# Projections from a normalised residual, in a new order of column blocks, in a two-layer hybrid block

## The chip, the cores and the metric

The kernel runs on one core of a Trainium2 chip. Its engines are TensorE (PE in the profile; PEld is its weight load), VectorE (DVE), ScalarE (ACT), GpSimd (POOL) and SyncE (SP), which here only issues transfers. The metric is the device time of one execution in microseconds; lower is better.

## The reference

Two layers, each with three token mixers side by side, then a gated feed-forward part, on 256 tokens of width 1024, all in float32. Cut to what matters:

```python
for l in range(2):
    h = rms_norm(x, norm_mix[l])              # x * rsqrt(mean(x*x) + 1e-6) * weight
    proj = h @ w_in[l]                        # 1024 -> 7688 columns
    (dq, dk, dv, dz, da, db, mq, mk, mv, lx, ly, gates) = split_columns(proj)
    # DeltaNet: conv4+silu on dq, dk, dv; chunked gated delta rule; rms_norm, times silu(dz)
    y_dn = gated_deltanet(dq, dk, dv, dz, da, db, ...) @ dn_out[l]
    y_mb = moba_attention(mq, mk, mv) @ mb_out[l]      # rope, causal softmax attention, 4 heads
    y_lru = rg_lru_branch(lx, ly, ...) @ lru_out[l]    # conv4, gates, linear scan, gelu(ly)
    g = sigmoid(gates + b_gate[l])                     # 3 x 1024 columns
    x = x + (g0 * y_dn + g1 * y_mb + g2 * y_lru) @ w_o[l]
    h = rms_norm(x, norm_ffn[l])
    gate, up = split(h @ ffn_in[l]);  x = x + (silu(gate) * up) @ ffn_down[l]
return rms_norm(x, norm_final)
```

## The kernel before

All weights come as one stream of 292 half blocks of 128 x 1024 float32 (512 KB each), 146 steps in each layer. A step k uses half block m = 146 l + k. Five buffers (`RING`) hold it raw; ACT rounds it to `whi` (`hi`, L676), DVE takes the rest into `wlo` (`lo`, L909), and PE makes three products (high x high, high x low, low x high). The activations are split the same way into `ahi` and `alo`. Both splits run four steps ahead (`AHEAD`): in step k, ACT and DVE prepare half block k + 4, and the buffer is free when PE is through with step k - 1.

Steps 0 to 59 of a layer are the input projection, two steps for each of 30 blocks of 256 columns. `by_output` (L292) keeps the weights stationary and streams 256 tokens: 24 matmuls of 128 x 256 in a step. `z_tokens` (L408; steps 32 to 35, the columns dz) keeps the tokens stationary and streams 512 columns: 12 matmuls of 128 x 512 in a step. Steps 60 to 71 are the three output products (y), 72 to 79 are w_o, 80 to 145 the feed-forward part, by tokens.

Nothing is scheduled by a tool: the order on each engine is written by hand. Each engine runs over the steps k, and a function `side(l, k)` holds what it does in step k besides the stream: on PE after the step's own matmuls, on ACT after rounding block k + 4, on DVE before `lo` of block k + 4. So one late operation holds back all that stands behind it on its engine, and also the weights of step k + 4.

The norm is applied late. PE projects x times the norm's weight; `evacuate` (L1038, the tensor operation at L1046) multiplies each pair of tiles by the tokens' reciprocal roots (`rstd`) on its way from PSUM to `proj`. The roots come from a sum of squares (`squares`, L707, on ACT) and `rsqrt` (L911, on DVE, with `settle()` waiting for each operation), and `norm_spread` (L431) spreads them over the partitions. Before layer 0, x comes transposed from memory (`xt_in`, `first_norm`); before layer 1, PE transposes it (`x_transpose`, L399) between the last matmuls of the layer ahead.

The DeltaNet work that the prediction speaks of, with its old steps: the column `conv` (L946) and silu of the six blocks of dq, dk, dv (`CONV_AT`); cumulative gates (`grow`, L1086, for PE in step 9); the table of decays E1 (differences at L1108, minimum, exponent at L729, steps 12 and 13); transposes of k and q and the squares of their rows (L737, steps 13 and 14); `kend` (L743, step 16); the inverse of the triangular matrix in five rounds of two products (`level`, `xcopy`, L1159, steps 18 to 27). The two products that give the attention its values by tokens are the transposes `mvT` (step 28).

Of the kernel before, what the change touches and what calls it, by code (L numbers as in the profile page):

```python
# [38 lines left out]

TQ, TK, TV, TMQ, TMK, TMV, TLX, TLY, TZ, TG = 0, 4, 8, 12, 16, 20, 24, 28, 32, 36  # L40
# [18 lines left out]
for _n, _k in [("ident", 128), ("causal", 128), ("fold", 8), ("cos", 256), ("sin", 256), ("tri", 128), ("eye", 64),  # L59
               ("up1", 64), ("up2", 64), ("up4", 64), ("up8", 64), ("up16", 64), ("up32", 64)]:  # L60
    CON[_n] = _at
    _at += _k
# [28 lines left out]
def build(nc, wstream, params, consts, norms, final, x_in, xt_in, ab_in, out, known):  # L91
    ctx = ExitStack()
    with ctx:
# [15 lines left out]
        con = sb("con", [P, NCON])  # L109
        par = sb("par", [P, NPAR])  # L110
        nrm = sb("nrm", [P, 2 * L * KT])
        rstd = sb("rstd", [P, T])
# [8 lines left out]
        small = sb("small", [P, 306])  # L121
# [5 lines left out]
        loaded_xt = [sem(f"loaded_xt{i}") for i in range(4)]  # L127
        loaded_x, loaded_final = sem("loaded_x"), sem("loaded_final")
# [5 lines left out]
        signals = (PE, DV, AC)  # L134
# [12 lines left out]
        for name, n in [("gcol", 8), ("bcol", 8), ("egc", 8), ("kes", 4), ("mx", 8), ("rs", 8),  # L147
                        ("brh", 4), ("bih", 4), ("bgh", 24), ("sp2", 4), ("sp4n", 4), ("nwh", 1), ("anex", 4), ("hr", 2), ("s2r", 2),
# [5 lines left out]
        assert at <= 306  # L154
# [20 lines left out]
        SQJ = 48  # L175
        PR, PT, VTOK = 48, 54, 8
        S1, WB, VN0, VN1, O1, OJ, OZ, ZT = 36, 16, 18, 38, 20, 8, 4, 4
        XC, TR, TI, A0, UU, HS = 12, 52, 0, 24, 20, 52
        MIX = 0
        XT, JUNK, FINAL, XW = 52, 44, TZ, 8  # L180
# [26 lines left out]
        CONV_AT = (5, 6, 7, 9, 11, 15)  # L207
# [17 lines left out]
        def in_bank(c):  # L225
            return bank[4 + c if c < 2 else c % 2]

        ZC = 16

        def is_z(k):  # L230
            return ZC <= k // 2 < ZC + 2

# [9 lines left out]
        def _(sp):  # L242
# [4 lines left out]

            sp.dma_start(nrm[:, :], norms).then_inc(loaded_nrm, 16)
            for p in range(4):
                sp.dma_start(tiles(XT + 2 * p, 2), xt_in[:, 2 * p:2 * p + 2, :]).then_inc(loaded_xt[p], 16)  # L250
                if p < 2:
                    load(p)
            sp.dma_start(rab[:, :, :, :], ab_in).then_inc(loaded_ab, 16)
            load(2)
            load(3)
            sp.dma_start(x[:, :, :], x_in).then_inc(loaded_x, 16)
            load(4)
            sp.dma_start(con[:, :], consts).then_inc(loaded_con, 16)
            for l in range(L):

                if l:
                    sp.wait_ge(*AC.at(l - 1, ("gates", 29)))
                    sp.wait_ge(*DV.at(l - 1, ("mixed", 3)))
# [7 lines left out]
            for t in (1, 0):  # L271
                for c in range(2):
                    sp.wait_ge(*(DV.at(L, ("out", t)) if c else AC.at(L, ("out", t))))
                    sp.dma_start(out[:, t, c * 512:(c + 1) * 512], x[:, t, c * 512:(c + 1) * 512]).then_inc(stored, 16)
# [4 lines left out]
        def _(pe):  # L279
# [12 lines left out]
            def by_output(l, k, dst, start_kt, act_wait=None):  # L292

                for i in range(4):
                    kt = start_kt + i
                    if act_wait is not None:
                        act_wait(kt)
# [92 lines left out]
            def turn_hidden(l, j):  # L390

                for t in range(2):
                    pe.wait_ge(*DV.at(l, ("hid", j, t)))
                    for f in range(2):
                        ins = pe.transpose(bank[3][:, f * T + t * P:f * T + (t + 1) * P],  # L395
                                           proj[:, HID + 2 * (j % 2) + t, f * P:(f + 1) * P], c_("ident", P))
                ins.then_inc(*PE.up(("hT", j)))

            def x_transpose(l, step, t):  # L399

                for c in range(2):
                    pe.wait_ge(*DV.at(l, (step, "x", t, c)))
                    for kt in range(4 * c, 4 * c + 4):
                        ins = pe.transpose(xt_of(kt)[:, t * P:(t + 1) * P], x[:, t, kt * P:(kt + 1) * P], c_("ident", P))
                        if kt % 2:
                            ins.then_inc(*PE.up((step, "xT", t, kt // 2), l))

            def z_tokens(l, k):  # L408

                m, q = l * NH + k, k - 2 * ZC  # L410
# [1088 lines left out]
```

## Time and profile before

| | us |
|---|---|
| median of 3 runs | 965.54 (964.45 to 967.15) |
| the profiled execution | 964.58, of it span 962.8 |
| PE busy | 935.2 (97% of the span), 6444 matmuls |
| DVE busy | 687.6 (71%) |
| ACT busy | 474.2 (49%) |
| POOL busy | 0.2 |
| weights and inputs read | 157.65 MB, 165 GB/s over the span |
| mean granted TensorE clock | 0.991 |

The chain of work that ended last goes 84% of its length through PE, 11% through DVE, 2% through ACT and 1% through a transfer. A row of a timeline has the start in us, the duration in us, the engine, the line and the operation with what it writes and reads; in brackets stands how long the engine had been idle and what ended that. Matmuls overlap, so their durations say little; their starts do.

### The profile page before, as it was taken

The numbers are of one execution on the slowest core, as the hardware profiler recorded it, in microseconds if no ns is written. First come the engines' busy times: TensorE is split into PE (matmuls) and PEld (weight loads), VectorE is DVE, ScalarE is ACT, GpSimd is POOL, SyncE is SP. The second block draws the span as 40 slices with busy tenths as digits, with TensorE's granted clock in tenths as the row PEclk, the third lists the DMA queues.
The fourth block names the chain that finished last, engine by engine and source line by source line (L and its number), as shares of the span: only waits on it lengthen the run. The fifth ranks groups of instructions, "written<-read, shape, count | busy, mean of one in ns | idle before, by whom it ended". The sixth has DMA issues, their size and how long they took to land.

```text
span 962.8 us, 15536 instructions
## 1 busy us (share of the span) xinstructions
PE 935.2 (97%) x6444; PEld 842.4 (87%) x6444; DVE 687.6 (71%) x1095; ACT 474.2 (49%) x769; POOL 0.2 (0%) x4
## 2 busy tenths in 40 slices
PE   7998999999999999999999899999999999999996
PEld 4998998999987888888889899999999788888884
DVE  4999976796777555555679998759758675565555
ACT  5554253975446444444454533558644464444442
POOL 0000000000000000000000000000000000000000
PEclk9999999999999999999999999999999999999998
DMA  9543433365564655565644343334655555555541
GB/s 339 169 139 131 133 109 115 130 194 199 167 196 147 210 180 197 175 204 187 201 137 132 126 133 132 123 120 135 215 189 181 178 196 197 181 183 187 180 145 44
DMA packets 44278, 159.71 MB, mean 166 GB/s; under 512 B 5040, under 2 KB 5168, under 8 KB 44080
## 3 DMA queue, kind: packets, MB, share of 16 engines
q1 hardware_dynamic: 44208, 158.72, 49.8%
q8 instruction: 51, 0.84, 0.4%
q14 instruction: 19, 0.16, 0.0%
HBM read 157.65 MB, written 1.05 MB: 165 GB/s over the span
## 4 chain that ended last, share of the span: by engine, by line
PE 84%; DVE 11%; ACT 2%; DMA 1%; issue 1%; SPq 0%; DVEq 0%; ACTq 0%
PE bank L282 11%; PE bank L283 10%; PE bank L284 10%; PE bank L382 8%; PE bank L380 8%; PE bank L381 8%; PE bank L429 6%; PE bank L322 5%; PE bank L323 5%; PE bank L324 5%; DVE tmp L952 3%; DVE wlo L909 3%; DMA x<-x_dram 1%; PE bank L395 1%; DVE proj L1046 1%; PE bank L418 1%
## 5 line engine op out<-in xcount | busy, mean ns | idle before, releaser
L676 ACT CAST whi<-raw 128x1024 fp32r<-128x1024 f32 x292 | 305.8, 1051 | 387.9 <-PE bank L284 152.6
L909 DVE TENSOR_TENSOR wlo<-raw,whi 128x1024 fp32r<-128x1024 f32 x292 | 353.5, 1219 | 115.8 <-ACT whi L676 115.7
L282 PE MATMUL bank<-ahi,whi 128*128 128x256 f32 x896 | 260.3, 291 | 0.7 <-DVE alo L977 0.6
L283 PE MATMUL bank<-alo,whi 128*128 128x256 f32 x896 | 254.7, 284 | 0.0
L284 PE MATMUL bank<-ahi,wlo 128*128 128x256 f32 x896 | 254.5, 284 | 0.0
L282 PEld LDWEIGHTS bank<-ahi,whi 128*128 128x128 f32 x896 | 173.1, 193 | 3.7 <-DVE alo L977 0.8
L283 PEld LDWEIGHTS bank<-alo,whi 128*128 128x128 f32 x896 | 173.2, 193 | 0.2
L284 PEld LDWEIGHTS bank<-ahi,wlo 128*128 128x128 f32 x896 | 173.0, 193 | 0.0
L380 PE MATMUL bank<-whi,ahi 128*128 128x512 f32 x320 | 126.5, 395 | 0.0
L382 PE MATMUL bank<-whi,alo 128*128 128x512 f32 x320 | 124.9, 390 | 0.0
L381 PE MATMUL bank<-wlo,ahi 128*128 128x512 f32 x320 | 124.6, 389 | 0.0
L382 PEld LDWEIGHTS bank<-whi,alo 128*128 128x128 f32 x320 | 60.1, 188 | 12.8
L381 PEld LDWEIGHTS bank<-wlo,ahi 128*128 128x128 f32 x320 | 60.2, 188 | 12.0
L380 PEld LDWEIGHTS bank<-whi,ahi 128*128 128x128 f32 x320 | 60.1, 188 | 11.9
L322 PE MATMUL bank<-whi,bhi 128*128 128x512 f32 x160 | 62.5, 390 | 0.0
L324 PE MATMUL bank<-whi,blo 128*128 128x512 f32 x160 | 62.3, 389 | 0.0
L323 PE MATMUL bank<-wlo,bhi 128*128 128x512 f32 x160 | 62.3, 389 | 0.0
L284 PE MATMUL bank<-bhi,wlo 128*128 128x256 f32 x192 | 54.4, 283 | 0.0
L282 PE MATMUL bank<-bhi,whi 128*128 128x256 f32 x192 | 54.3, 283 | 0.0
L283 PE MATMUL bank<-blo,whi 128*128 128x256 f32 x192 | 54.3, 283 | 0.0
L1352 DVE TENSOR_TENSOR blo<-bank,bhi 128x512 fp32r<-128x512 f32 x22 | 15.2, 692 | 40.3 <-ACT bhi L867 40.3
L1345 DVE SCALAR_TENSOR_TENSOR proj<-proj,bank 128x256 f32<-128x256 f32 x44 | 18.4, 418 | 35.4 <-ACT proj L863 35.4
(248 smaller groups left out, 1212.2 us busy)
## 6 DMA issues: line engine op xcount, KB each, us to landing
raw<-stream_dram SPq DMA_DIRECT2D x292, 512.0 KB, 4.0
par<-params_dram SPq DMA_DIRECT2D x2, 568.5 KB, 9.7
proj<-xt_dram SPq DMA_DIRECT2D x4, 256.0 KB, 6.3
x<-x_dram SPq DMA_DIRECT2D x1, 1024.0 KB, 10.6
out_dram<-x SPq DMA_DIRECT2D x4, 256.0 KB, 2.6
con<-consts_dram SPq DMA_DIRECT2D x1, 676.0 KB, 12.3
proj<-final_dram SPq DMA_DIRECT2D x1, 512.0 KB, 6.1
rab<-ab_dram SPq DMA_DIRECT2D x1, 64.0 KB, 7.4
```

Of the source, the lines that this page charges most:

```text
L282: pe.matmul(dst, whi_of(m)[:, wcol], hi, start=first, stop=False, skip_group_check=True)
L283: pe.matmul(dst, whi_of(m)[:, wcol], lo, start=False, stop=False, skip_group_check=True)
L284: return pe.matmul(dst, wlo_of(m)[:, wcol], hi, start=False, stop=last, skip_group_check=True)
L322: pe.matmul(dst, hi[:, tok], whi_of(m)[:, col], start=first, stop=False, skip_group_check=True)
L323: pe.matmul(dst, hi[:, tok], wlo_of(m)[:, col], start=False, stop=False, skip_group_check=True)
L324: ins = pe.matmul(dst, lo[:, tok], whi_of(m)[:, col], start=False, stop=False, skip_group_check=True)
L380: pe.matmul(dst, ahi[:, kt, tok], whi_of(m)[:, col], start=kt == 0, stop=False, skip_group_check=True)
L381: pe.matmul(dst, ahi[:, kt, tok], wlo_of(m)[:, col], start=False, stop=False, skip_group_check=True)
L382: ins = pe.matmul(dst, alo[:, kt, tok], whi_of(m)[:, col], start=False, stop=kt == KT - 1, skip_group_check=True)
L429: return pe.matmul(dst, lhsT, rhs, start=start, stop=stop, skip_group_check=True)
L676: act.copy(whi_of(m), raw_of(m)).then_inc(*AC.up(("hi", m), "w"))
L909: dv.tensor_tensor(wlo_of(m), raw_of(m), whi_of(m), ALU.subtract).then_inc(*DV.up(("lo", m), "w"))
```

## The change

- The order of blocks in the stream changes. z comes first (steps 0 to 3), then the blocks in the order of `AT`: dk, mq, dk, mq, dq, mk, dq, mk, dv, ly, dv, then mv (steps 26 to 29), lx, ly, lx and the gates. Blocks that feed a convolution alternate with blocks that don't.
- z and mv are computed by tokens. z goes through all four steps for tokens 0 to 127 and then for tokens 128 to 255. The eight transposes `mvT` are dropped.
- x is multiplied by its reciprocal root before it is transposed and split (`root`, `x_scaled`, `mix_norm`), in both layers, one half of the tokens after the other. `rstd`, `norm_spread` and the multiplication in `evacuate` are dropped; so is the transposed copy of x in memory. The root's Newton steps use one operation less each.
- With no scaling left, projections are read from PSUM by their consumers: the taps and the convolution, the gates' tanh, and plain copies by ACT (`in`, L842 of the new kernel).
- The products for da, db move from step 1 to step 3. Most side steps move: kk stays at 15, qT from 13 to 20, qk from 16 to 21, vT from 17 to 28, the inverse starts at 19 for 18, attention scores go from 26 to 31, the LRU part shifts by some five steps.
- The table of decays: ACT subtracts (eight activations with a bias), GpSimd sets what is above the diagonal (`affine_select`), then ACT takes the exponent. The copies `xcopy`, `xn` and the state go from DVE to ACT.
- The end: each half's root has its own chain, and the halves' stores change order.

```diff
+ROOT = -1.0 / 8192
+MV0 = 26
+CONVS, LX = (2, 3, 0, 1, 4, 5), (12, 13)
+AT = {2: 4, 6: 6, 3: 8, 7: 10, 0: 12, 8: 14, 1: 16, 9: 18, 4: 20, 14: 22, 5: 24, 12: 30, 15: 32, 13: 34}
+AT.update((c, 2 * c) for c in range(18, 30))
+FM = sorted(AT, key=AT.get)
-        CONV_AT = (5, 6, 7, 9, 11, 15)
+        CONV_AT = tuple(AT[c] + 2 for c in CONVS)
+            def z_tokens(l):
+                for t in range(2):
+                    for q in range(4):
+                        if t == 0:
+                            wait_split(l, q)
+                        ins = token_half(l, q, q, t, bank[4 + t][:, :])
...
+                        if t == 0 and q == 2:
+                            x_transpose(l, "mix", 1)
...
                     elif c < C_IN:
-                        if c > 3 and half == 0:
-                            pe.wait_ge(*DV.at(l, ("zs", c - ZC - 2) if ZC + 2 <= c < ZC + 4 else ("evac", c - 2)))
+                        n = FM.index(CHUNK[c])
+                        if n > 1 and half == 0:
+                            by, name = in_copied(FM[n - 2])
+                            pe.wait_ge(*by.at(l, name))
+            def mix_norm(l):
+                for c in range(2):
+                    if l == 0:
+                        act.wait_ge(loaded_x[0], 16)
+                    else:
+                        act.wait_ge(*DV.at(l, ("mix", "x", 0, c)))
+                    square(l, 0, c)
+                hi(l * NH + AHEAD - 1 if l else 0)
+                x_scaled(l, 0)
+                x_round(l, "mix", 2 * l, 0, (0, 1))
...
                 if k == 12:
-                    act.wait_ge(*DV.at(l, "dif"))
-                    act.activation(wide(E1, 4), wide(E1, 4), ACT.Exp).then_inc(*AC.up())
...
+                    act.wait_ge(*PE.at(l, "gbc"))
+                    for g in range(8):
+                        act.activation(wide(E1, 4)[:, g, :], b3(4 + g // 4, 4)[:, g % 4, :], ACT.Identity, bias=sm["gneg"][:, g:g + 1]).then_inc(*AC.up("dif"))
+                if k == 13:
+                    act.wait_ge(*PO.at(l, "causal"))
+                    act.activation(wide(E1, 4), wide(E1, 4), ACT.Exp).then_inc(*AC.up("decays"))
+            def root(l, t, order=(0, 1)):
...
+                for three in (3.0, 12.0, 768.0):
+                    settle()
+                    step(dv.scalar_tensor_tensor(out=u, in0=y, scalar=w, in1=y, op0=ALU.mult, op1=ALU.mult))
+                    settle()
+                    step(dv.scalar_tensor_tensor(out=y, in0=u, scalar=-three, in1=y, op0=ALU.add, op1=ALU.mult), ("mix", "nr", t))
-            def evacuate(l, k):
...
-                    step(dv.tensor_tensor(tiles(2 * c, 2), in_bank(c)[:, :].rearrange("p (a b) -> p a b", a=2),
-                                          over(rstd[:, :], 2), ALU.mult), ("evac", c))
+        @block.gpsimd
+        def _(po):
+            for l in range(L):
+                PO.layer = l
+                po.wait_ge(*AC.at(l, "dif"))
+                po.affine_select(wide(E1, 4), wide(E1, 4), [[0, 8], [1, P]], ALU.is_ge, -1e4, base=0, channel_multiplier=-1).then_inc(*PO.up("causal"))
```

The three places of the order on which the prediction leans. First ACT at the very start, before: L687 is the split of the transposed x, L708 the squares.

```order
L687 ACT_TABLE_LOAD
L687 ACTIVATE ahi<-proj,nrm 128x256 x2
L676 CAST whi<-raw 128x1024
L687 ACTIVATE ahi<-proj,nrm 128x256 x2
L676 CAST whi<-raw 128x1024
L687 ACTIVATE ahi<-proj,nrm 128x256 x4
L676 CAST whi<-raw 128x1024 x2
L708 ACTIVATE proj,small<-x 128x1024 x2
L676 CAST whi<-raw 128x1024
L714 CAST wab<-rab 128x8x8
```

The squares stood behind the split of x; nothing but the small product waited for them. The same place now: L710 squares, L724 x times its root, L719 the split.

```order
L710 ACT_TABLE_LOAD
L710 ACTIVATE proj,small<-x 128x512 x2
L707 CAST whi<-raw 128x1024
L724 ACTIVATE proj<-x,small 128x512
L719 ACTIVATE ahi<-bank,nrm 128x128 x2
L707 CAST whi<-raw 128x1024
L719 ACTIVATE ahi<-bank,nrm 128x128 x4
L707 CAST whi<-raw 128x1024
L719 ACTIVATE ahi<-bank,nrm 128x128 x2
L710 ACTIVATE proj,small<-x 128x512 x2
L707 CAST whi<-raw 128x1024
L724 ACTIVATE proj<-x,small 128x512
```

Now the squares and the root stand ahead of all the splits. Second, ACT around steps 12 to 15 of a layer, before: L729 the exponent, L737 the squares of the rows of k and q, L763 a tap.

```order
L729 ACTIVATE proj<-proj 128x1024
L730 ACTIVATE small<-small 128x4
L731 ACTIVATE small<-small 128x8
L676 CAST whi<-raw 128x1024
L737 ACTIVATE proj,small<-bank 128x128 x8
L676 CAST whi<-raw 128x1024
L737 ACTIVATE proj,small<-bank 128x128 x8
L763 ACTIVATE tmp<-proj,par 128x256 x2
L676 CAST whi<-raw 128x1024
```

The same place now: L808 the differences, L842 a copy of a block, L812 the exponent, L818 squares, L778 a tap, L804 the tanh of a convolution.

```order
L808 ACTIVATE proj<-bank,small 128x128 x8
L809 ACTIVATE small<-small 128x8
L842 COPY proj<-bank 128x512
L707 CAST whi<-raw 128x1024
L812 ACTIVATE proj<-proj 128x1024
L818 ACTIVATE proj,small<-bank 128x128 x8
L778 ACTIVATE tmp<-bank,par 128x256 x2
L707 CAST whi<-raw 128x1024 x2
L804 ACTIVATE tmq<-tmp 128x512
```

The exponent waits for GpSimd, and the taps of the third convolution stand behind it. Third, POOL in the new kernel, with what its rows wait for; in the old one it has only the first rows, up to the memsets.

```order
L1553 MEMSET const-uint8-127 128x1
L1446 UNCONDITIONAL_BRANCH [waits barrier_Pool_Activation_PE_DVE_SP_gather]
L1451 ISA [waits scalar_done]
L1451 AFFINE_SELECT proj<-proj 128x1024
L1451 AFFINE_SELECT proj<-proj 128x1024 [waits scalar_done]
L102 UNCONDITIONAL_BRANCH
```

One row without a tensor (ISA; in the built program it asks for the engine's library of functions) stands between the first wait for ACT and the first select, layer 0's. Layer 1's select has none ahead of it.

## Rows read from the trace of the kernel before

**Rows 1.** Who waited for whom on PE: total, times, longest, in us.
```profile
PE bank L446 <- DVE wab L1052: 4.7, 1, 4.7
PE bank L429 <- ACT Kend L743: 4.4, 2, 2.9
PE bank L429 <- DVE small L1086: 3.6, 2, 1.8
...
PE bank L429 <- DVE proj L1159: 1.2, 1, 1.2
```

**Rows 2.** Stretches: length, each engine's busy time and instructions, granted clock, DMA share, GB/s.
```profile
8.91:30.16 21.25, 16.50 (x121) 14.73 (x119) 13.86 (x34) 11.98 (x18) 0.00 (x0) 0.92 0.90 357
30.16:87.17 57.01, 53.69 (x459) 53.08 (x458) 54.22 (x128) 32.35 (x83) 0.00 (x0) 0.97 0.40 127
30.16:272.77 242.61, 238.06 (x2143) 232.26 (x2143) 200.72 (x329) 125.50 (x232) 0.00 (x0) 0.99 0.45 148
500.56:743.36 242.80, 238.04 (x2144) 232.37 (x2143) 200.74 (x329) 125.52 (x232) 0.00 (x0) 0.99 0.45 147
190.00:270.00 80.00, 80.00 (x669) 80.00 (x668) 62.26 (x70) 43.63 (x54) 0.00 (x0) 1.00 0.57 187
332.00:347.00 15.00, 15.00 (x68) 12.41 (x67) 9.06 (x11) 6.58 (x9) 0.00 (x0) 1.00 0.55 179
```

**Rows 3.** Groups by line and shape: count, then busy us, mean ns, idle before.
```profile
L909 DVE TENSOR_TENSOR wlo<-raw,whi 128x1024 fp32r<-128x1024 f32 x292 | 353.5, 1219 | 115.8 <-ACT whi L676 115.7
L1046 DVE TENSOR_TENSOR proj<-bank,rstd 128x512 f32<-128x512 f32 x56 | 38.2, 685 | 6.5 <-PE bank L284 6.2
...
L952 DVE SCALAR_TENSOR_TENSOR tmp<-proj,par,tmp 128x255 f32<-128x255 f32 x24 | 10.5, 480 | 0.0
...
L438 PE MATMUL bank<-con,proj 128*128 128x128 f32 x80 | 10.5, 274 | 0.0
```

**Rows 4.** Timeline of ACT: the first 20 us, then eight squares of step 13.
```profile
4.20 1.28 ACT L687 ACT_TABLE_LOAD   x1 [4.20 <-DMA proj<-xt_dram]
...
6.55 1.05 ACT L676 CAST whi<-raw 128x1024 fp32r<-128x1024 f32 x1 [0.15 <-DMA raw<-stream_dram]
...
16.55 1.06 ACT L708 ACTIVATE proj<-x 128x1024 f32<-128x1024 f32 x1 [1.44 <-DMA x<-x_dram]
...
66.13 0.27 ACT L737 ACTIVATE proj<-bank 128x128 f32<-128x128 f32 x1
...
67.89 0.31 ACT L737 ACTIVATE proj<-bank 128x128 f32<-128x128 f32 x1
```

**Rows 5.** Timeline of DVE: masks and first transpose of step 16; a root's chain.
```profile
79.37 1.78 DVE L1139 TENSOR_TENSOR proj<-bank,proj 64x256 f32<-64x256 f32 x4
...
84.40 2.32 DVE L909 TENSOR_TENSOR wlo<-raw,whi 128x1024 fp32r<-128x1024 f32 x2
...
493.40 0.16 DVE L914 TENSOR_SCALAR small<-small 128x2 f32<-128x2 f32 x1
...
495.38 0.16 DVE L923 SCALAR_TENSOR_TENSOR small<-small 128x2 f32<-128x2 f32 x1
```

**Rows 6.** Timeline of PE where layer 0 ends and layer 1 begins.
```profile
480.20 0.39 PE L337 MATMUL bank<-whi,blo 128*128 128x512 f32 x1
...
486.28 0.36 PE L282 MATMUL bank<-ahi,whi 128*128 128x256 f32 x1 [0.62 <-DVE alo L977]
```

**Rows 7.** Timeline of ACT at the square root of the LRU part.
```profile
190.59 1.28 ACT L830 ACT_TABLE_LOAD   x1
191.88 1.06 ACT L830 ACTIVATE proj<-proj 128x1024 f32<-128x1024 f32 x1
```

**Rows 8.** The page, DMA issues: count, KB each, median us to landing.
```profile
raw<-stream_dram SPq DMA_DIRECT2D x292, 512.0 KB, 4.0
```

**Rows 9.** Timeline of DVE at the end of the program.
```profile
954.84 0.16 DVE L1010 TENSOR_TENSOR small<-small 128x2 f32<-128x2 f32 x1 [0.26 <-ACT proj L887]
...
957.50 1.41 DVE L1027 SCALAR_TENSOR_TENSOR x<-x,small,proj 128x512 f32<-128x512 f32 x2
```

More of the change, by code:

```diff
@@ L270, in _ @@
                         sp.dma_start(flat(tiles(FINAL, 4)), final).then_inc(loaded_final, 16)
[L271 to L274, printed above, removed]
+            for t, c in ((0, 0), (1, 0), (1, 1), (0, 1)):
+                sp.wait_ge(*(DV.at(L, ("out", t)) if c else AC.at(L, ("out", t))))
+                sp.dma_start(out[:, t, c * 512:(c + 1) * 512], x[:, t, c * 512:(c + 1) * 512]).then_inc(stored, 16)
             sp.wait_ge(stored, 64)
@@ L707, in squares, with ffn_norm, wab_hi @@
+            def ffn_norm(l):
+                for t in range(2):
+                    x_round(l, "ffn", 2 * l + 1, t, range(KT))
+                for t in range(2):
+                    squares("ffn", t)
+            def wab_hi(l):
+                if l == 0:
+                    act.wait_ge(loaded_ab, 16)
+                act.copy(wab[:, :, 0:8], rab[:, l, :, :]).then_inc(*AC.up("wabh"))
             def squares(step, t):
@@ new lines, in x_scaled, with mix_update, add @@
+            def x_scaled(l, t):
+                settle()
+                step(dv.tensor_scalar(flat(tiles(XS + 4 * t + 2, 2)), x[:, t, 512:D], sm["nr"][:, t:t + 1], None, ALU.mult), ("xs", t))
+            def mix_update(l):
+                def add(t, c):
+                    if l:
+                        x_add(l, "mix", NH - 1, t, c)
+                add(0, 0)
+                add(0, 1)
+                root(l, 0)
+                x_scaled(l, 0)
+                if l == 0:
+                    lo(0)
+                add(1, 0)
+                x_split(l, "mix", 2 * l, 0, (0, 1))
+                if l == 0:
+                    lo(1)
+                add(1, 1)
+                x_split(l, "mix", 2 * l, 0, (2, 3, 4, 5))
+                if l == 0:
+                    lo(2)
+                x_split(l, "mix", 2 * l, 0, (6, 7))
+                root(l, 1)
+                x_scaled(l, 1)
+                lo(l * NH + AHEAD - 1)
+                x_split(l, "mix", 2 * l, 1, range(KT))
@@ L1025, in last_update @@
[L1025 to L1028 removed]
+                root(L, 1, (1, 0))
+                weighed(1)
+                weighed(0)
             def rnorm(l, name):
@@ L1189, in side @@
                                                      in1=Vb[:, 2 * h + 1, :], op0=ALU.mult, op1=ALU.add), "w")
-                if k == 36:
-                    for t in range(2):
-                        dv.wait_ge(*AC.at(l, ("tz", t)))
-                        step(dv.scalar_tensor_tensor(out=flat(tiles(TZ + 2 * t, 2)), in0=flat(tiles(ZT + 2 * t, 2)), scalar=1.0,
-                                                     in1=bank[t][:, :], op0=ALU.add, op1=ALU.mult), ("zs", t))
-                if k == 37:
+                if k == 38:
                     dv.wait_ge(*PE.at(l, "qs"))
```

678 lines of the change are left out of this document (328 added, 350 removed), and 2 rows, old and new, of the table at.

## The prediction

> **What bounds the kernel now.** I read the page first: PE is busy for 935.2 of 962.8 us, so time can only come from fewer matmuls or from the 27 us in which PE stands. Then the waits of PE [rows 1]. They are few and all lie in the two norms and in steps 4 to 19: 4.7 us at the very start (the products for da, db, behind the squares of x), 3.6 in two waits on `grow`, 4.4 in two on `Kend` (1.5 in layer 0, 2.9 in layer 1), 1.2 on one `xcopy`. Third, stretches [rows 2]. From step 4 to w_o a layer takes 242.6 and 242.8 us. Its first part, to step 19, is where DVE is busy 54.2 of 57.0 us: there DVE sets the pace, in the rest PE does. The granted clock is 1.00, full speed, in the stretches where PE never stops (190 to 270, 332 to 347), 0.97 in the early steps and 0.92 at the start, where PE had stood for those 4.7 us. What a clock of c costs in a stretch is (1 - c) of its length: 1.7 us in each of these two. Last the pace: 669 matmuls of 256 columns in 80 us, 0.120 each, 2.9 us for a step of 24; 68 matmuls of 512 columns in 15 us, about 0.225, 2.7 us for a step of 12 [rows 2].
>
> **PE's work.** mv by tokens: four steps at 2.7 for 2.9, -0.6 us a layer with rounding. The eight transposes `mvT` go; 80 such took 10.5 us [rows 3], eight with their filling some 0.9. The fold of da, db comes from step 3 into the stretch after step 4 (+0.5). So a layer's stretch from step 4 has 0.9 us less of pure work.
>
> **DVE's and ACT's work.** DVE loses `evacuate`, 28 x 0.68 = 19 us a layer [rows 3], and three kinds of copies to ACT. Where DVE sets the pace (steps 4 to 18) nine of them go, 6.1 of 54 us, and about 2 more with the differences, so the two `grow` waits should go. It helps only if DVE waits for nothing else, so I walk both engines through the new order, in us from the start of step 4, signals at zero cost. A `lo` is 1.2, a convolution of six operations 2.5 [rows 3], a block's copy by ACT 0.6, a rounding 1.0; eight squares take 2.0 (67.89 less 66.13 is seven of them [rows 4]); masks and first transpose 5.0 [rows 5].
> Up to step 12, nothing waits: convolution 0 ends at 9.6 and is wanted at 12.1, the log chain ends at 14 and is wanted at 20.8. PE starts step 12 at 24.8, 13 at 28.5, 14 at 31.4, 15 at 34.3, 16 at 38.9, 17 at 41.8, 18 at 44.7, 19 at 47.6, and would start 20 at 51.6. ACT has the differences at 27.1. Then GpSimd's select takes P. The exponent (1.0), eight squares (2.0) and the taps of step 14 (0.8) stand behind it on ACT, so with P = 2 the taps are there at 32.9, 1.5 after the block they read. Behind them on DVE stand convolution 2 (to 35.4), rope and `lo` (37.6), the scaling of the decays (39.4) and `lo` (40.6), silu, rope and `lo` (43.5), the masks (48.5), `lo`, convolution 3 (52.0), rope and two `lo`, silu 3 (56.0). PE wants convolution 2 at 38.9, the masks' transpose at 50.5, convolution 3 at 51.6 and silu 3 for the transposes of q at 54.5. So PE waits 0.4 + 1.1 = 1.5 us. DVE makes none of it up, since its `lo` is bound to the step that runs. The same walk with P = 4, 6, 8 gives 3.7, 5.6, 7.5: from 2 on, each us of select costs PE almost a us. From step 21 on I find no wait up to w_o; the closest places are the last round of the inverse (step 27: ready at 85.6, wanted at 86.3) and the square root, below.
>
> **What P is.** No row of this trace has GpSimd at work on a tile. The lower end is ACT's own pass over 1024 columns, 1.06 us [rows 4]; I take 2 us, since DVE's pass of two operands is 1.2 [rows 3] and GpSimd is not likely to be ahead of it, and for the upper end 4.0, the next larger thing there is to compare with, a transfer's landing [rows 8]. In layer 0 the order shows a row between the wait and the select that asks for the engine's functions. If they are fetched there, that is a transfer at the least, and I price it at 4.0 us, one landing [rows 8], from 0 to twice that. So P is 6 in layer 0 and 2 in layer 1. The Trainium skill, GPSIMD Engine Reference, "Instruction dispatch", says that the first call of a freshly loaded function pays about 6 us with nothing in the profile to show it. By it P would be 8 in layer 0 and the sum 1.9 us higher. No run here shows it yet.
>
> **The stretch from step 4, by layer.** Layer 0: gone are 1.8 + 1.5 + 1.2 of waits and 1.7 of clock, 6.2; work -0.9; new waits 5.6 by the walk and 1.0 for the signals that I took at zero. Sum -0.5. Layer 1: gone are 1.8 + 2.9 and some 1.5 of clock, 6.2; work -0.9; new waits 1.5 + 1.0. Sum -4.6.
>
> **The start, to step 4.** Before it is at 30.16. Now x's first half (512 KB for the 256 KB that had landed at 4.20) comes at some 4.4; table load 1.3 and two squares 0.7 each to 7.1; the root, eight operations of 0.2 (ten took 495.38 - 493.40 = 1.98 [rows 5]), to 8.8; scaling 0.6, four transposes, the rounding and rest of the first tile: first product at 10.8, before at 8.91. PE then waits for the blocks: rounding and rest of blocks 1, 2, 3, which land at about 11, 12.8 and 14, stand between the splits of x, so z's first half ends at 20.6. The second half is ready by then and takes 5.5, the products for da, db 1.9: step 4 at 28.0. The 4.7 us wait is gone (it came from x landing at 16.5 [rows 4]), but PE stands about 5 us in pieces between 12 and 19; I add 1.0 for the clock. Sum -1.2, between -2.2 and +2.
>
> **Between the layers.** The last product of x's first half starts at 480.20 and PE starts layer 1 at 486.28, step 4 at 500.56 [rows 6, 2]. Now: second add to 481.5, square 482.3, root 484.0, scaling and four transposes 485.1, first tile split 485.9; the three quarter passes of z end at 490.05; the second half's scaled x is there at 490.9, its transposes end at 491.8, z's first half at 493.3, the second at 498.8, da and db at 500.7. That is +0.1, with PE standing 2.3 before the first product and 0.9 later. I add 0.7 for clock. Sum +0.8, from 0 to +3. What hid the norm before was that only its root was late; now the root is in front of every product.
>
> **The end.** The root of the later half waited for the last square, 954.84 to 957.50, both halves in one chain, and two stores of DVE followed to 958.9 [rows 9]. One chain of eight operations is 1.6 for 2.7, but the order of the last two additions puts its last square 0.6 later, and the first half's store goes early. Sum -0.9, from -1.3 to 0.
>
> **The square root: a rule that speaks against the change.** ACT had table load, root and rounding in step 43 and the load back in 44. Now both loads and the tanh of block 23 stand in step 48: 1.0 + 1.3 + 1.0 + 1.3 + 0.85 = 5.45 us, and PE wants that block's bank after 2 x 2.9 = 5.8. It fits by 0.3, since the root starts 0.01 us after its load ends [rows 7]. The Trainium skill, ScalarE: Activation LUTs, "What ACT_TABLE_LOAD costs", gives 1.28 us plus a drain of 1.38 for each switch; by it the step would be 8.2 us and PE would wait 2.4 in each layer. The trace has the 1.28 and not the drain.
>
> **Sum.** -1.2 - 0.5 + 0.8 - 4.6 - 0.9 = -6.4. The profiled execution is 964.58, so 958.2; the median of the runs is 0.96 higher, so 959.1.
>
> **The rivals.**
> 1. The functions are there already and P is 2 in both layers. Layer 0 then gains what layer 1 does: 4.1 more, 955.0. For it: POOL's memsets run at once at the program's start. Against: the row behind the wait.
> 2. GpSimd is slow in itself. Should the select take 8 us in both layers, PE waits 7.5 + 1.0 in layer 1 and, with the fetch, 11.4 + 1.0 in layer 0: 6.0 + 5.8 on the forecast, 970.9, slower. It decides from a select of about 7 us. For it: no row bounds it. Against: two other engines pass over such a tile in 1.1 and 1.2.
> 3. DVE keeps its backlog: PE-to-ACT-to-DVE hops cost more than my 1 us, and each of the six convolutions, which now holds a PSUM bank, makes PE wait. With 4 us a layer, 965: no change. For it: half of PE's old waits were of this kind, and DVE had no idle time in those steps. Against: 8 us less of DVE work there.
> 4. Each switch of table costs ACT its load twice over, 2 x 1.28: step 48 becomes 8.0 us, PE waits 2.2 in each layer, 4.4 more, 963.5. Against: [rows 7]. The Trainium skill's drain, on the page named above, would make it 4.9 more.
> 5. The walk is too dark and all the early waits go, 951 to 953.
>
> **How the numbers follow.** Forecast 0.43, rival 1 0.28, rival 2 0.08, rival 3 0.12, rival 4 0.03, rival 5 0.06. A measurement tells 0.3%, 2.9 us, from no change. Faster: forecast, rivals 1 and 5, 0.77. Same: rivals 3 and 4 but for 0.01, 0.14. Slower: rival 2 and that 0.01, where clock and waits fall worse, 0.09. The range takes in rivals 1 and 3 and the low clock at both starts: 952 to 966; the forecast's own is 956 to 962.
>
> **What would show it.** POOL gets two rows on `proj`; the first one's start minus the end of the eighth difference on ACT is the fetch, its length the rest of P. PE should wait on convolution 3 or the taps' chain in step 16 to 20, more in layer 0. `grow` and `Kend` are gone from PE's waits. ACT's step 48 should end before PE's step 50. Step 4 starts near 29 and, in layer 1, 21 us after the last addend. I am wrong if PE still loses 6 us in early steps of layer 1, or if both layers' stretches come out alike.

## The result, and the profile after

The kernel before takes 965.31 us (median of 4 runs, 964.45 to 967.15), the new one 951.69 (951.40 to 952.00): a ratio of 0.9856, 95% interval 0.9839 to 0.9874. That is 13.6 us less. I had forecast 6.4 less, 959.1, with a range down to 952.0: the direction was right, the size half of what came, and the time lies just under the range. The profiled execution went from 964.58 to 952.00, its span from 962.8 to 950.2. I had forecast 958.2 for it, so 6.2 us of the miss lie in the execution itself; the rest is that I added 0.96 for the median, as in the kernel before, while the new kernel's median lies 0.31 under its profiled execution.

First the stretches of the new kernel, to be laid beside [rows 2]. Columns: length, busy time of PE, PE's weight loads, DVE, ACT and POOL with their instructions, granted clock, share of the DMA engines, GB/s.

```profile
1.45:28.34 26.89, 23.52 (x93) 16.07 (x93) 18.79 (x47) 18.74 (x40) 0.00 (x0) 0.94 0.85 301
28.34:84.14 55.80, 54.86 (x481) 54.26 (x479) 47.10 (x97) 31.92 (x67) 1.09 (x1) 1.00 0.49 162
28.34:265.43 237.09, 236.09 (x2141) 229.92 (x2139) 177.52 (x287) 132.23 (x250) 1.09 (x1) 1.00 0.47 153
475.54:494.36 18.82, 16.75 (x83) 13.34 (x82) 15.02 (x41) 13.43 (x32) 0.00 (x0) 0.91 0.25 81
494.36:731.43 237.07, 236.09 (x2140) 229.93 (x2139) 177.52 (x287) 132.20 (x250) 1.09 (x1) 1.00 0.47 153
940.89:950.20 9.31, 0.39 (x2) 0.00 (x0) 5.63 (x19) 2.67 (x6) 0.00 (x0) 0.80 0.30 113
```

Step 4 starts at 28.34 and 494.36, w_o at 265.43 and 731.43, the last product at 940.89. So the 12.6 us of the profiled execution divide like this:

| part | before | after | measured | forecast |
|---|---|---|---|---|
| start to step 4 | 30.16 | 28.34 | -1.8 | -1.2 |
| layer 0, step 4 to w_o | 242.61 | 237.09 | -5.5 | -0.5 |
| w_o of layer 0 to step 4 of layer 1 | 227.79 | 228.93 | +1.1 | +0.8 |
| layer 1, step 4 to w_o | 242.80 | 237.07 | -5.7 | -4.6 |
| w_o of layer 1 to the end | 219.44 | 218.77 | -0.7 | -0.9 |

Five of the 6.2 us that I missed are in one row, layer 0; 1.1 more are in layer 1. In each layer PE's idle time (length less busy) went from 4.55 and 4.76 us [rows 2] to 1.00 and 0.98, and its busy time from 238.06 and 238.04 to 236.09. The new kernel's early steps run at the full clock (1.00, before 0.97) with DVE busy 47.1 of 55.8 us (before 54.2 of 57.0).

The waits of PE, beside [rows 1]: total, times, longest.

```profile
PE bank L420 <- ACT proj L724: 4.4, 3, 1.5
PE bank L469 <- DVE proj L1177: 1.6, 2, 0.8
PE bank L466 <- DVE tmp L1422: 1.5, 1, 1.5
PE bank L420 <- DVE x L1037: 1.4, 2, 0.7
PE bank L431 <- DVE alo L1045: 1.1, 2, 0.5
PE bank L404 <- DVE proj L1412: 0.4, 1, 0.4
```

None of the waits that I had counted in the layers [rows 1] is left, nor the 4.7 us at the start. L724 is the scaling of x at the two norms, L469 the transposes of q in step 20, which stand behind the silu of the fourth convolution: the only wait in a layer from step 4 to w_o, 0.8 us each time. L466, the second L420 (on x) and L404 had their like in the kernel before.

Then the place where my largest term stood, GpSimd's select, and ACT around it in layer 0. Columns: start, length, engine, line, operation, and what ended the idle time before it.

```profile
55.91 1.09 POOL L1451 TENSOR_SCALAR_AFFINE_SELECT proj<-proj 128x1024 f32<-128x1024 f32 x1 [55.47 <-ACT small L809]
521.83 1.09 POOL L1451 TENSOR_SCALAR_AFFINE_SELECT proj<-proj 128x1024 f32<-128x1024 f32 x1 [464.82 <-ACT small L809]
```
```profile
53.51 2.17 ACT L808 ACTIVATE proj<-bank,small 128x128 f32<-128x128 f32 x8
55.52 0.26 ACT L809 ACTIVATE small<-small 128x8 f32<-128x8 f32 x1
55.62 0.64 ACT L842 COPY proj<-bank 128x512 f32<-128x512 f32 x1
56.30 1.05 ACT L707 CAST whi<-raw 128x1024 fp32r<-128x1024 f32 x1
57.26 1.05 ACT L812 ACTIVATE proj<-proj 128x1024 f32<-128x1024 f32 x1
```

The differences end at 55.68 (53.51 + 2.17) and the small exponent behind them at 55.78; the select starts at 55.91 and takes 1.09 us, in layer 1 the same. It ends at 57.00, while ACT copies a block and rounds weights until its next row at 57.26: the exponent does not wait for GpSimd. P, from the end of the eighth difference to the end of the select, which I took as 6 in layer 0 and 2 in layer 1, was 1.3, and hidden.

### The profile page after: what moved, and what is told of

It is laid out like the page before. It is cut to its first block, busy times and chain, and to the rows that moved or that the text cites. A ratio compares the mean times of both kernels' runs of the same rounds, so it can differ in the third digit from the quotient of the medians.

```text
span 950.2 us, 15345 instructions
## 1 busy us (share of the span) xinstructions
PE 930.6 (98%) x6344; PEld 833.7 (88%) x6344; DVE 646.4 (68%) x1026; ACT 495.0 (52%) x837; POOL 2.4 (0%) x6
## 3 DMA queue, kind: packets, MB, share of 16 engines
HBM read 156.60 MB, written 1.05 MB: 166 GB/s over the span
## 4 chain that ended last, share of the span: by engine, by line
PE 88%; DVE 7%; ACT 3%; DMA 1%; issue 1%; SPq 0%; DVEq 0%; ACTq 0%
PE bank L293 12%; PE bank L294 11%; PE bank L295 11%; PE bank L391 8%; PE bank L389 8%; PE bank L390 8%; PE bank L466 6%; PE bank L333 5%; PE bank L331 5%; PE bank L332 5%; PE bank L431 2%; DVE wlo L984 2%; PE bank L432 1%; PE bank L433 1%; PE bank L404 1%; DVE tmp L1031 1%
## 5 line engine op out<-in xcount | busy, mean ns | idle before, releaser
L293 PE MATMUL bank<-ahi,whi 128*128 128x256 f32 x832 | 239.5, 288 | 0.4
L294 PE MATMUL bank<-alo,whi 128*128 128x256 f32 x832 | 235.3, 283 | 0.0
L295 PE MATMUL bank<-ahi,wlo 128*128 128x256 f32 x832 | 235.3, 283 | 0.0
L293 PEld LDWEIGHTS bank<-ahi,whi 128*128 128x128 f32 x832 | 159.4, 192 | 2.0 <-DVE tmp L1031 0.5
L294 PEld LDWEIGHTS bank<-alo,whi 128*128 128x128 f32 x832 | 159.5, 192 | 0.1
L295 PEld LDWEIGHTS bank<-ahi,wlo 128*128 128x128 f32 x832 | 159.4, 192 | 0.0
```

The costliest lines, as they stand in the source:

```text
L293: pe.matmul(dst, whi_of(m)[:, wcol], hi, start=first, stop=False, skip_group_check=True)
L294: pe.matmul(dst, whi_of(m)[:, wcol], lo, start=False, stop=False, skip_group_check=True)
L295: return pe.matmul(dst, wlo_of(m)[:, wcol], hi, start=False, stop=last, skip_group_check=True)
```

## The experiments

What a stretch is worth is read off each profile as above; the two profiles of the new kernel agree within 0.03 us in the stretches from step 4. Here all of them (start is the time of step 4; between is w_o of layer 0 to step 4 of layer 1):

| kernel | start | layer 0 | between | layer 1 | span | median | ratio to before, 95% |
|---|---|---|---|---|---|---|---|
| new | 28.3 | 237.1 | 228.9 | 237.1 | 950.2 | 951.69 | 0.9839 to 0.9874 |
| new, again | 28.5 | 237.1 | 228.2 | 237.1 | 949.7 | 951.65 | 0.9851 to 0.9879 |
| three and five selects | 28.9 | 241.6 | 228.2 | 243.0 | 960.5 | 962.04 | 0.9962 to 0.9983 |
| selects at the start too | 28.2 | 237.1 | 229.0 | 237.1 | 950.0 | 951.85, one run | none |
| mask on DVE | 29.3 | 237.1 | 229.0 | 237.1 | 951.3 | 952.55 | 0.9852 to 0.9890 |
| copies on DVE | 28.5 | 237.7 | 228.2 | 237.7 | 950.9 | 953.24 | 0.9860 to 0.9896 |
| inverse's copies on DVE | 28.9 | 237.4 | 228.2 | 237.4 | 950.6 | 952.50 | 0.9862 to 0.9892 |
| pairs adjacent | 28.9 | 236.6 | 228.2 | 236.6 | 949.2 | 950.89 | 0.9849 to 0.9878 |
| q one step later | 28.3 | 236.1 | 228.2 | 236.0 | 947.3 | 949.17 | 0.9830 to 0.9863 |
| filling | 28.3 | 237.1 | 228.2 | 237.1 | 949.4 | 951.45 | 0.9855 to 0.9884 |
| filling, q later | 29.0 | 236.1 | 228.2 | 236.1 | 948.2 | 949.56 | 0.9831 to 0.9859 |
| before, six copies on ACT | 29.5 | 239.7 | 227.8 | 239.7 | 956.1 | 959.06 | 0.9918 to 0.9956 |

### Is there a fetch of code? Selects at the program's start

```
 def _(po):
+    spare = wide(56, 4)
+    po.memset(spare, 0.0)...
+    po.wait_ge(*PO.last())
+    po.affine_select(spare, spare, ...)...
+    po.wait_ge(*PO.last())
+    po.affine_select(spare, spare, ...)...
     for l in range(L):
```

> The new kernel with a memset and two selects of a spare tile on GpSimd at the very start of the program, 128x1024 each, where nothing can hide a fetch of code. Theory A (GpSimd needs no time to get the select's code): the first select starts within 0.3 us of the memset's end and takes 1.1 like the others. Theory B (there is a fetch, hidden in the 55 us in which GpSimd waited in the new kernel): the first one starts some 4 to 6 us after the memset or takes that much longer, the second follows at once.

POOL's first rows:

```profile
0.73 0.95 POOL L1450 MEMSET proj<- 128x1024 f32 x1 [0.29 <-POOLq L1560]
1.92 1.09 POOL L1452 TENSOR_SCALAR_AFFINE_SELECT proj<-proj 128x1024 f32<-128x1024 f32 x1 [0.23 <-POOL proj L1450]
3.15 1.09 POOL L1454 TENSOR_SCALAR_AFFINE_SELECT proj<-proj 128x1024 f32<-128x1024 f32 x1
```

Theory A. The first select of the program starts 0.23 us behind the memset and takes the 1.09 of every other; the second starts 0.14 behind the first. Only 1.9 us of program lie ahead of it, too few to hide a fetch of 4 to 6 us. Whether the functions had been loaded before the execution began is not shown; the four timed executions of the new kernel lie within 0.6 us of each other (951.40 to 952.00), and the profiled one, which shows no fetch, is the longest of them, so none of the four paid for one.

### Was the walk right? The select made longer

```
-    po.affine_select(wide(E1, 4), wide(E1, 4), ...)
+    for i in range((3, 5)[l]):
+        if i:
+            po.wait_ge(*PO.last())
+        po.affine_select(wide(E1, 4), wide(E1, 4), ...)
```

> The new kernel with GpSimd's select run three times over in layer 0 and five times in layer 1, so that it takes 3.3 and 5.5 us where one took 1.1. My theory (the walk of the prediction was right, only its 4 us of fetch did not happen): the chain exponent, squares, taps behind the select is what PE waits for, and every us from 2 on costs PE almost one. In the new kernel the exponent starts 1.35 us after the select's start in any case, since a copy and a rounding of ACT lie beside it; so the exponent comes 1.9 us later in layer 0 and 4.1 in layer 1, and the stretch from step 4 to w_o, 237.1 in both, becomes some 238.8 (+1.5 to +1.9) and 240.9 (+3.6 to +4.1); the whole +5 to +6 us. Rival A (the walk was too dark, there is slack behind the select): less than 0.5 in layer 0 and under 2 in layer 1, the whole under +2.5.

```profile
56.48 4.36 POOL L1454 TENSOR_SCALAR_AFFINE_SELECT proj<-proj 128x1024 f32<-128x1024 f32 x3 [56.04 <-ACT small L809]
526.21 6.83 POOL L1454 TENSOR_SCALAR_AFFINE_SELECT proj<-proj 128x1024 f32<-128x1024 f32 x5 [465.37 <-ACT small L809]
```
```profile
60.88 1.06 ACT L812 ACTIVATE proj<-proj 128x1024 f32<-128x1024 f32 x1 [2.95 <-POOL proj L1454]
533.08 1.06 ACT L812 ACTIVATE proj<-proj 128x1024 f32<-128x1024 f32 x1 [5.33 <-POOL proj L1454]
```

A select that waits for the one before costs more than its 1.09, so P is 4.4 and 6.8, not the 3.3 and 5.5 that I had written. From the select's start to the exponent it is now 4.40 and 6.87 us where it was 1.35 (57.26 - 55.91), so the exponent is 3.05 and 5.52 later. The stretches grew by 4.5 and 5.9, the time by 10.4: so rival A (slack behind the select) is out, and a late select does cost PE. The parts of it, in three stretches (the two layers', then a piece of layer 0) and in PE's timeline there:

```profile
28.91:270.49 241.58, 238.41 (x2141) 232.38 (x2140) 178.09 (x287) 131.98 (x250) 4.07 (x3) 0.99 0.46 150
498.73:741.73 243.00, 237.67 (x2140) 231.47 (x2139) 178.06 (x287) 131.90 (x250) 6.26 (x5) 0.99 0.46 150
80.00:86.00 6.00, 3.30 (x42) 3.19 (x43) 6.00 (x11) 2.27 (x4) 0.00 (x0) 0.71 0.29 95
```
```profile
80.31 1.15 PE L466 MATMUL bank<-Tm,proj 64*64 64x64 f32 x32 [0.72 <-DVE Tm L1223]
83.85 0.55 PE L293 MATMUL bank<-ahi,whi 128*128 128x256 f32 x1 [2.39 <-DVE tmp L1031]
84.20 0.41 PE L294 MATMUL bank<-alo,whi 128*128 128x256 f32 x1
84.41 0.41 PE L295 MATMUL bank<-ahi,wlo 128*128 128x256 f32 x1
```

Idle time is 3.2 and 5.3 us where it was 1.0, so the waits grew by 2.2 and 4.3 for delays of 3.05 and 5.52. My walk gives 3.2 and 5.5 for these delays, counted from P of 2: its level is about 1 us too dark, its slope (0.95 us of wait for a us of delay) near the measured one (2.1 for 2.5). And busy time grew by 2.3 and 1.6 with the same work: behind the wait of 2.39 the next 24 matmuls come 0.21 apart, not 0.12 (84.20 to 84.41), half the clock (1.2 GHz for 2.4) for a whole step, as the granted clock of that piece says (0.50):

```profile
83.85:89.11 5.26, 5.26 (x25) 5.26 (x26) 5.26 (x6) 2.42 (x4) 0.00 (x0) 0.50 0.49 152
```

With P at 4.4 layer 0 still gains 1.0 us over the kernel before (242.61 to 241.58). Between the two layers' rows (241.58 at 4.4, 243.00 at 6.8) a P of 6 comes to some 242.5, an estimate: -0.1 where I had forecast -0.5. So with a select that long the forecast for the layer would have been close.

### Has DVE room? The mask as an addition on DVE

```
+    if k == 13:
+        dv.wait_ge(*AC.at(l, "dif"))
+        step(dv.tensor_tensor(wide(E1, 4), wide(E1, 4), over(c_("late", P), 8), ALU.add), "causal")
-    po.affine_select(wide(E1, 4), wide(E1, 4), ...)
```

> The new kernel with the select replaced by an addition of a table on DVE (1.2 us, 128x1024), in step 13. Theory A (DVE has room there): DVE waits 2.4 us for the third convolution's taps just behind that place, so the addition lies in idle time; the exponent comes 0.3 to 0.6 later and each layer loses 0.5 at most, the whole under +1. Theory B (DVE's busy time sets the pace of the early steps, as I read it from the kernel before): all of the 1.2 shows, +1.2 a layer, +2.4 in the whole.

Both stretches are 237.1, unchanged to 0.03 us; of the span's 1.1 more, 1.0 is the start (29.3), where weights and x land. The addition falls where DVE has nothing to do, and DVE still waits for the taps of the third convolution behind it, 1.82 us for 2.4:

```profile
56.66 1.23 DVE L1175 TENSOR_TENSOR proj<-proj,con 128x1024 f32<-128x1024 f32 x1 [0.85 <-ACT proj L808]
...
62.09 2.43 DVE L1031 SCALAR_TENSOR_TENSOR tmp<-bank,par,tmp 128x255 f32<-128x255 f32 x6 [1.82 <-ACT tmp L778]
```

So having GpSimd do this is worth nothing by itself: the mask could stay with DVE. Theory B, DVE's sum as the pace, no longer holds; for the kernel before it is tested below, with one part alone.

### Which of the moved copies count?

```
 # six blocks without convolution; then, in a kernel of its own, the five copies in the inverse
-    act.copy(flat(tiles(2 * c, 2)), in_bank(c)[:, :])...
+    step(dv.tensor_copy(flat(tiles(2 * c, 2)), in_bank(c)[:, :]), ("in", c))
...
-    act.copy(mat(XM), b3(4, 8))...
+    step(dv.tensor_copy(mat(XM), b3(4, 8)), ("xcopy", i))
```

> The new kernel with the copies of the six blocks without convolution made by DVE again in place of ACT (about 0.6 to 0.7 each, four of them in steps 8 to 20). Theory A (what counts is the one chain from the taps of the third convolution to the silu of the fourth): the copies of steps 8 and 12 fall into DVE's idle time, the one of step 16 lies in the chain: +0.7 a layer, the one of step 20 another 0.3, the whole +1.4 to +2. Theory B (DVE's sum sets the pace): four times 0.68 a layer, +2.7, the whole +5.4.

> The new kernel with the five copies inside the inverse (steps 20 to 28) on DVE again in place of ACT, about 0.68 each. Theory A (only a copy that stands behind the silu of step 20 is late): the first copy comes some 0.5 after PE wants it, the other four are hidden by steps of 2.9: +0.3 to +0.6 a layer, the whole +0.6 to +1.2. Theory B (moving them was worth what PE had waited on them before, 1.2 in one layer, and more, since DVE has no room): +1.2 or more a layer, the whole +2.4.

The first costs 0.65 us a layer: theory A, with a new wait of 0.7 on the fourth convolution, just ahead of step 20. The second costs 0.27 a layer. That is the lower end of theory A (0.3 to 0.6), but its reason is not borne out: the first copy is not late, since the product behind it starts 62.74 us after step 4 (91.66 - 28.92) where it was 62.75 (91.09 - 28.34). The loss comes in pieces of about 0.1 from the inverse's product of step 24 on (75.33 for 75.19).

```profile
PE bank L469 <- DVE proj L1173: 0.8, 1, 0.8
PE bank L293 <- DVE tmp L1027: 0.7, 1, 0.7
```

(Waits of PE in the first of the two, from step 4 to w_o of layer 0.) Undone one at a time, these parts cost 0.3 to 0.7 of the 5.6 us a layer that the whole change gives: with the other parts in place, each of them matters little.

### One part alone, on the kernel before

```
 # blocks 0 to 5 (q, k, v): copied by ACT ahead of the rounding of the same step
+    act.copy(tiles(2 * c, 2), in_bank(c)...)
-    if ZC <= c < ZC + 2:
+    if ZC <= c < ZC + 2 or c < 6:      # DVE skips these blocks
         continue
```

> The kernel before with one part of the change alone: the blocks of q, k and v (six of 28) are copied out of PSUM by ACT, not by DVE; the copy leaves out the multiplication with the norm. DVE loses 6 x 0.68 = 4.1 us a layer, all in steps 4 to 12, ACT gets 6 x 0.6. Theory A (DVE sets the pace of steps 4 to 19, so its work is PE's time): the stretch from step 4 to w_o, 242.6 and 242.8, loses 3 to 4 us a layer, the whole -6 to -8; that would be most of what the change gave in the layers (-5.5 and -5.7). Theory B (only the waits on the log chain go, and what waits for ACT stays): -1.8 a layer, the whole -3 to -4, with the waits on Kend still there.

The copy leaves out the norm's multiplication for these six blocks, so the kernel computes something else and serves only as a measure of time. -2.9 and -3.1 us a layer, -5.3 in the time (964.33 to 959.06): between the two theories, nearer to A in the layers, and with B's wait on `Kend` still there. Idle time fell from 4.55 and 4.76 to 1.97 in both layers, all of it on `Kend`: the waits on the log chain (`small`) and on `xcopy` are gone, and the wait for ACT is now the same 2.0 in both. PE's busy time fell by 0.3 only, and the early clock is still 0.97.

```profile
29.49:269.18 239.69, 237.72 (x2144) 232.27 (x2144) 197.29 (x323) 127.70 (x236) 0.00 (x0) 0.99 0.46 150
```
```profile
PE bank L429 <- ACT Kend L748: 2.0, 1, 2.0
```

DVE's busy time fell by 3.4 (200.72 to 197.29; the six durations of 0.68 overlap a little), and that gave 2.9 and 3.1, about half of the layers' gain: so DVE did set the pace there. What is missing to the new kernel in layer 0 is 2.6 us (239.69 to 237.09), 1.0 of it idle time, with the 2.0 on `Kend` gone and the 0.8 in step 20 come, and 1.6 busy time, the slower clock and some work. In the new kernel the product behind `Kend` stands five steps later (21 for 16), and neither the wait nor the slow clock is there. That the one took the other away is not shown: which of its edits brings the clock back was not run by itself.

### The order of the convolutions

```
-AT = {2: 4, 6: 6, 3: 8, 7: 10, 0: 12, 8: 14, 1: 16, 9: 18, ...}
+AT = {2: 4, 3: 6, 6: 8, 7: 10, 0: 12, 1: 14, 8: 16, 9: 18, ...}
```

> The new kernel with the blocks of q and k next to each other again (two convolutions in steps 6 and 8, two in 14 and 16, not every fourth step), the plain blocks behind each pair. The work of each engine is the same. Theory A (the order counts for the chain in front of the transposes of q only): the second convolution of q is ready earlier, the wait of 0.8 in step 20 goes, the masks of step 17 come some 2 us later with 1 us or so of cover: between -1 and +1 a layer. Theory B (alternation keeps DVE from falling behind, two convolutions of 2.4 and two splits of 1.2 do not fit into two steps of 2.9 with anything beside them): +2 or more a layer.

236.6 in both layers, 0.45 less than with the pairs apart: theory A. The wait in step 20 is gone, and one of 0.4 to 0.5 on the second convolution has come. So the alternation of convolutions with plain blocks, a part of the change, gives nothing here.

### The last wait of a layer: q one step later

```
-    if k == 20:   # PE, transposes of q
+    if k == 21:
-    if k in (13, 21):   # ACT, squares
+    if k in (13, 22):
```

> The new kernel with the eight transposes of q and their squares one step later (21 and 22 for 20 and 21). Theory A (the 0.8 us that PE waits in each layer for the silu of step 20 is lost time): it goes, -0.8 to -1.0 a layer, the whole -1.6 to -2. Theory B (PE meets the next late thing, the level or copy of the inverse behind the same DVE work): the wait reappears under another name, the whole within 0.4.

-1.04 us a layer; the median goes from 951.69 to 949.17. Theory A. The list of PE's waits from step 4 to w_o is empty, and PE is busy for 235.88 of 236.05 us:

```profile
28.27:264.32 236.05, 235.88 (x2140) 229.94 (x2139) 177.31 (x287) 131.91 (x250) 1.09 (x1) 1.00 0.48 154
```

### The clock at the two norms: filling, and the new kernel again

```
-    for i in range(6):   # warm-up products
+    for i in range(7):
...
+    fill = con[:, 0:512] if l else tmp[:, 0, :]
+    if l:
+        exact(bank[3][:, :], ident[:, :], fill)
     x_transpose(l, "mix", 0)
+    exact(bank[4][:, 0:T], ident[:, :], fill[:, 0:T])
```

> The new kernel with idle matmuls where PE stands at the two norms: a seventh warm-up product at the start, one of 512 columns where layer 1 begins, and one of 256 columns between the transposes and the first product of z in both. Results go to banks that the next product overwrites. In the new kernel the first seven products of z run at the lower clock in both places (0.43 us each for 0.23), 1.4 us each time. Theory A (the clock fell because PE stood, and keeping it busy keeps it up): those products take 0.23, -1.0 to -1.4 at each place, the whole -2 to -3. Theory B (z's first products run slow whatever stood before them, or the filling delays the transposes by what it saves): within 0.5.

> The new kernel with both edits together: the transposes of q one step later, and idle matmuls where PE stands at the two norms. Each alone gave -2.9 and -0.8 of the span (the second only where the clock had fallen between the layers: with full clock z's first half still waits for the scaled second half of x, the same 228.2 from w_o to step 4). Theory A (they are apart and add, but the filling has nothing left to give in a run whose clock stayed up): 947.2 to 948.3 as profiled, the stretches from step 4 at 236.05. Theory B (the filling shortens the start too, where the clock always fell): a us less, 946.

> The new kernel itself once more, beside the version with both edits. A second profile tells whether the 228.9 us from w_o to step 4 of layer 1 in the first one was the clock's doing: theory A (yes) 228.2 with z's first products at 0.23 us, theory B (the new kernel's own) 228.9 again. Time 951 to 952.

In the new kernel's first profile PE comes out of the norm between the layers at half clock (0.43 us from product to product, 479.65 to 481.79; full again at 482.50):

```profile
477.46 1.09 PE L420 MATMUL bank<-ident,proj 128*128 128x128 f32 x8 [1.53 <-ACT proj L724]
479.09 0.77 PE L431 MATMUL bank<-whi,ahi 128*128 128x512 f32 x1 [0.54 <-DVE alo L1045]
479.65 0.63 PE L432 MATMUL bank<-wlo,ahi 128*128 128x512 f32 x1
...
482.50 0.39 PE L433 MATMUL bank<-whi,alo 128*128 128x512 f32 x1
```

With the filling the products follow at 0.23 from the start, and then PE stands for the scaled second half of x:

```profile
479.31 0.39 PE L432 MATMUL bank<-wlo,ahi 128*128 128x512 f32 x1
479.54 0.39 PE L433 MATMUL bank<-whi,alo 128*128 128x512 f32 x1
...
483.86 1.10 PE L420 MATMUL bank<-ident,proj 128*128 128x128 f32 x8 [0.53 <-ACT proj L728]
```

The clock is up, as theory A has it, and the time is theory B's. But the filling need not be what held the clock up: the second profile of the new kernel, without any filling, has z's products at 0.23 there too and the same 228.2 us:

```profile
477.65 1.09 PE L420 MATMUL bank<-ident,proj 128*128 128x128 f32 x8 [1.54 <-ACT proj L724]
479.28 0.47 PE L431 MATMUL bank<-whi,ahi 128*128 128x512 f32 x1 [0.54 <-DVE alo L1045]
479.59 0.39 PE L432 MATMUL bank<-wlo,ahi 128*128 128x512 f32 x1
479.82 0.40 PE L433 MATMUL bank<-whi,alo 128*128 128x512 f32 x1
```

The same holds for all eleven profiles of the new kernel and its variants: the three that read 228.9 to 229.0 have the slow products between the layers, the eight that read 228.2 have not, and only two of the eight are filled. At the program's start four of the nine without filling have them, which I had taken for the rule, and they reach step 4 no later (28.2 to 28.9 against 28.3 to 29.3). So the clock there changes from one execution to the next: two profiles of the same kernel differ in it. It is worth 0.7 us between the layers and nothing at the start, where I take the landings of x and the weights to decide, which no run tested. Between the layers, with the clock up, what bounds the place is the chain add, square, root and scaling of x's second half. Filling alone gains nothing (951.45 for 951.69), and neither does it on top of the later q (949.56 for 949.17, and 2.1 us under the new kernel run beside it, 951.65): theory A of that run, the stretches at 236.07 and the span at 948.2. The version with q one step later is the best one run, 0.3% under the new kernel; the two were timed apart, each beside the kernel before, and their intervals overlap, so the 0.3% rests on the stretches of the profiles and on the version with filling.

## Why the prediction was right in direction and wrong in size

**Layer 0 from step 4, the step that failed.** Forecast -0.5, measured -5.5: new waits 6.6 forecast, 1.00 of idle time measured, less 0.6 of the busy time that I had expected to go. The term was P of 6 us: a fetch of 4.0, priced at a transfer's landing from one row in the order without a tensor, and 2 for the select. Measured: no fetch, a select of 1.09, and both under ACT's own copy and rounding, which stood in the order between the differences and the exponent and which my walk did not set against P. The run with selects at the start shows that no fetch was hidden in the wait. The sign that I had named came too: both layers' stretches are alike, 237.09 and 237.07. Rival 1, no fetch, was the case that came (I gave it 0.28 and 955.0). By the Trainium skill, GPSIMD Engine Reference, "Instruction dispatch", the first call of a freshly loaded function pays about 6 us. The trace does not bear it out for this instruction: the first select of the program stands 0.23 us behind the memset. The doubt had its place in the range; what was wrong was to make the unseen cost the likeliest value.

**What is removed.** 6.2 us a layer of waits and clock was right: the old waits of 4.5 and 4.7 are all gone, and the early clock is back at 1.00.

**PE's work.** I took 0.9 less. Busy time fell by 1.97 in layer 0 and 1.95 in layer 1, and I had put 1.7 and 1.5 of it to the clock; so the work fell by 0.3 to 0.5, and I was some 0.5 too rosy a layer. The term at fault is the 0.6 for mv by tokens. Counted from step 4 to w_o of layer 0, before and after, the products by tokens are as many as they were:

```profile
L418 PE MATMUL bank<-whi,ahi 128*128 128x512 f32 x16 | 6.5, 406 | 0.0
L431 PE MATMUL bank<-whi,ahi 128*128 128x512 f32 x16 | 6.7, 416 | 0.0
```

Before, they were z's (steps 32 to 35), now they are mv's, and z has gone ahead of step 4. What is saved there is saved in steps 0 to 3, where my walks of the start and of the place between the layers had it already. Without the 0.6 my own terms give -0.9 for the transposes and +0.5 for the fold, -0.4, which is what came.

**New waits.** In layer 1 I had 1.5 from the walk and 1.0 for signals, 2.5; measured 0.98 of idle time, 0.8 of it where the walk put 1.1 (silu and transposes of q in step 20). The 1.0 for the signals was mis-sized, it did not come. 1.5 better here and 0.45 worse in busy time (1.95 for 2.4) are the 1.1 that layer 1 gave more than forecast. The walk's slope stands by the run with more selects (2.1 of wait for 2.5 of delay), but for the half clock behind a wait of 2.4 us, which was not in it.

**The start.** -1.8 for -1.2: within the spread of 28.2 to 29.3 that the eleven profiles with this start have.

**Between the layers.** +1.1 for +0.8 in this profile, +0.4 in most: the chain, for which I had +0.1, costs 0.4, and the 0.7 for the clock is what it costs when it is down. That this profile came near the forecast is partly luck, since the clock was down in three of eleven.

**The end.** -0.7 for -0.9.

**The square root.** It fits, with the loads back to back and PE's wait on it nil: rival 4 is out.

```profile
197.36 1.28 ACT L909 ACT_TABLE_LOAD   x1
198.65 1.06 ACT L909 ACTIVATE proj<-proj 128x1024 f32<-128x1024 f32 x1
199.73 1.28 ACT L925 ACT_TABLE_LOAD   x1
```

**The other rivals.** GpSimd slow in itself (rival 2) needed a select of 7 us; it takes 1.09. DVE's backlog (rival 3, 4 us of new waits a layer) is out: the new waits are 1.0, and DVE takes on 1.2 us more of mask at no cost to the stretches. Rival 5 (all early waits go, 951 to 953) has the time, but not the mechanism: one wait of 0.8 was left, and taking it away gave another us a layer.

## What to carry to other kernels

A cost that the trace does not show belongs into the range, not into the likeliest value, unless a row bears it out; and a delay on one engine is first laid against what that engine's successor does anyway. Where an engine is busy for 95% of a stretch, as DVE was here, the first few us taken from it can bring the gain (3.4 gave 3.0) and parts taken beyond that little (0.3 to 0.7 when undone); undo the parts one by one before believing in each. After such a relief read the waits again: the one that was left here was mended by moving eight transposes one step, for a us a layer.

## What the runs showed that I had not expected

- Behind a wait of 2.4 us PE ran a whole step of 24 matmuls at the lower clock, 0.21 us each for 0.12; that alone cost 2.3 us, as much as the wait. Behind a wait of 1.65 us in layer 1 of the same run the clock stayed at 1.00.
- GpSimd's select over 128x1024 takes 1.09 us, a memset 0.95, as fast as ACT's pass of 1.05; one that waits for the one before it starts 1.2 to 1.6 us behind the start of that one.
- In two profiles of one and the same kernel the clock was down between the layers in one and not in the other, while the stretches from step 4 repeat to 0.03 us.
